# Attention on one core: four heads scored earlier, masks and normalising on GpSimd, half of the key copy by DMA

## The reference

```python
proj = h @ w_in
oa = _dilated_attention(...)            # heads 0-7: softmax of q k^T / 8 - slope * distance + log(count)
# heads 8-15, in blocks of 128 queries
sc = jnp.einsum("bhqe,bhke->bhqk", q_i, k) * (dh ** -0.5)
sc = sc + c_i[..., None] - c[:, :, None, :]
sc = jnp.where(kpos[None, :] <= qpos[:, None], sc, -jnp.inf)
p = jax.nn.softmax(sc, axis=-1)
o = jnp.einsum("bhqk,bhke->bhqe", p, vf)
return jnp.concatenate([oa, ob], axis=-1) @ w_out
```

## Time and profile before

| | us |
|---|---|
| median of 3 runs | 1294.28 (1294.25 to 1295.91) |
| the profiled execution | 1295.59 |
| its span in the trace | 1293.8 |
| TensorE busy | 1254.6 (97%) |
| VectorE busy | 936.4 (72%) |
| ScalarE busy | 769.2 (59%) |
| GpSimd busy | 294.9 (23%) |
| mean granted clock of TensorE | 0.989 |

### The profile page before, as it was taken

The page is one execution under the profiler, slowest core; times in us unless marked ns, Lnnn a source line. Parts: engine busy times, 40 slices in busy tenths (PEclk is TensorE's granted clock), DMA queues, the critical chain, the costliest instruction groups (busy, mean ns, idle before and its releaser), DMA issues.

```text
span 1293.8 us, 19412 instructions
## 1 busy us (share of the span) xinstructions
PE 1254.6 (97%) x7446; PEld 1101.4 (85%) x7446; DVE 936.4 (72%) x1223; ACT 769.2 (59%) x1064; POOL 294.9 (23%) x303
## 2 busy tenths in 40 slices
PE   9988986899999999999999999999999999999997
PEld 6766775689899898998989889898889899898996
DVE  6366447569967859588866697657799876959678
ACT  6666465347757456576546564646668746557564
POOL 2554341011122111220222121142212221111220
PEclk9999998999999999999999999999999999999999
DMA  7355446577899898996586867968598999898983
GB/s 249 83 115 122 122 106 138 136 207 198 193 218 222 216 233 202 219 202 207 112 206 148 227 140 209 210 136 191 154 239 182 215 230 232 214 231 183 218 220 102
DMA packets 148492, 238.96 MB, mean 185 GB/s; under 512 B 51616, under 2 KB 73384, under 8 KB 148400
## 3 DMA queue, kind: packets, MB, share of 16 engines
q0 software_dynamic: 32352, 102.79, 42.2%
q1 hardware_dynamic: 115744, 134.60, 33.2%
q10 hardware_dynamic: 304, 0.33, 0.1%
HBM read 127.57 MB, written 2.11 MB: 100 GB/s over the span
## 4 chain that ended last, share of the span: by engine, by line
PE 87%; DVE 6%; ACT 2%; issue 2%; DMA 1%; POOL 1%; SPq 0%; DVEq 0%; ACTq 0%; POOLq 0%
PE bank L899 21%; PE bank L931 18%; PE bank L1306 11%; PE bank L1374 6%; PE pv L931 5%; PE bank L1256 5%; PE pv L899 4%; PE bank L1097 4%; PE bank L1037 3%; PE bank L1198 2%; PE bank L1064 2%; DVE arena L2250 1%; PE bank L1270 1%; PE bank L1320 1%; PE pv L1320 1%
## 5 line engine op out<-in xcount | busy, mean ns | idle before, releaser
L2167 DVE TENSOR_TENSOR w<-raw_tiles,w 128x1024 fp32r<-128x1024 f32 x312 | 371.5, 1222 | 90.9 <-ACT w L1516 90.8
L1516 ACT ACTIVATE w<-raw_tiles 128x1024 fp32r<-128x1024 f32 x312 | 315.2, 1051 | 123.8 <-PE bank L931 59.9
L3080 POOL DMA_DIRECT2D raw_tiles<-raw_tiles x176 | 152.2, 907 | 629.3 <-DVE w L2167 376.3
L899 PE MATMUL bank<-h_ops,w 128*128 128x256 f32 x2304 | 281.4, 283 | 0.0
L899 PEld LDWEIGHTS bank<-h_ops,w 128*128 128x128 f32 x2304 | 278.9, 192 | 0.7
L931 PE MATMUL bank<-w,arena_q 128*128 128x512 f32 x1044 | 241.5, 390 | 0.0
L931 PEld LDWEIGHTS bank<-w,arena_q 128*128 128x128 f32 x1044 | 195.2, 188 | 40.5 <-DVE x L2469 0.3
L1306 PE MATMUL bank<-w,h_ops 128*128 128x512 f32 x624 | 144.0, 390 | 0.0
L1306 PEld LDWEIGHTS bank<-w,h_ops 128*128 128x128 f32 x624 | 116.6, 188 | 24.0
L1097 PE MATMUL bank<-hT_hi,w 128*128 128x512 f32 x224 | 78.5, 401 | 0.1
L1735 ACT ACTIVATE arena<-arena,negmax 128x512 f32<-128x512 f32 (+1 forms) x64 | 35.9, 561 | 58.4 <-DVE negmax L2250 58.0
(11 more groups left out here) (252 smaller groups left out, 1836.4 us busy)
## 6 DMA issues: line engine op xcount, KB each, us to landing
raw_tiles<-raw_tiles POOLq DMA_DIRECT2D x176, 512.0 KB, 5.5
raw_tiles<-in_ffn_w_in SPq DMA_DIRECT2D x64, 512.0 KB, 5.6
raw_tiles<-in_ffn_w_out SPq DMA_DIRECT2D x64, 512.0 KB, 6.4
raw_tiles<-in_odd_w_in SPq DMA_DIRECT2D x32, 512.0 KB, 5.4
raw_tiles<-in_even_w_in SPq DMA_DIRECT2D x48, 256.0 KB, 3.3
raw_tiles<-in_odd_w_in SPq DMA_DIRECT2D x32, 256.0 KB, 5.4
raw_tiles<-in_odd_w_out SPq DMA_DIRECT2D x16, 512.0 KB, 6.0
raw_tiles<-raw_tiles POOLq DMA_DIRECT2D x20, 256.0 KB, 4.4
```

What stands on the lines that cost most here:

```text
L899: mm = pe.matmul(bank[first + b][:, 256 * m:256 * m + 256], w_slots[use_slot(use)][:, p, k, c:c + P], h_ops[:, H_BLOCK[op], q, k, :], star ...
L1516: nc.scalar.activation(w_flat(use_slot(use), 0, half), raws[tile][:, 1024 * half:1024 * half + 1024], ACT.Copy).then_inc(m_hi, 1)
L2167: nc.vector.tensor_tensor(w_flat(use_slot(use), 1, half), raws[use_tile(key)][:, 1024 * half:1024 * half + 1024], w_flat(use_slot(use), 0, ...
L3080: pool.dma_start(raws[dst][:, part], raws[src][:, part], accum_op=ALU.add).then_inc(t_made[value][half], 16)
```

## The change

- **Steps.** Heads 8 to 11 are scored beside jobs 16 to 19, head 12 right behind its key job 22, so two heads instead of three are left to the tail.
- **Buffers.** Two of `rden` and of the output `o_sb`; heads 13 and 15 have part and turned buffers of their own (`OWN`); `v_rest` has a place for each group; the mask of the first block goes to `first_block`.
- **Masks and normalising** move from VectorE to GpSimd, but for the last pair. The factor 1/P_SCALE moves to the output's high and low part.
- **Key copy.** For pairs 0 to 5 ScalarE writes each head's own half, and two DMAs on SP's queue write the other half. The first score unit of a head waits for them (`key_copied`).
- **Order in a step.** VectorE makes the first logits before the parts and the output's low part last. TensorE turns the output at piece 5 instead of 0.
- **`early_split`** would put a weight split between the exponentials; it returns False for every job.

```diff
-         15: [(None, 7, 6, 2)],
-         16: [(None, None, 7, None)],
-         17: [(None, None, None, 3)],
-         18: [(8, None, None, None)],
-         19: [(9, 8, None, None)],
-         21: [(10, 9, 8, None)],
-         22: [(11, 10, 9, None)],
-         23: [(12, 11, 10, 4)],
-         24: [(13, 12, 11, None), (14, 13, 12, 5), (15, 14, 13, None)]}
+         15: [(8, 7, 6, 2)],
+         16: [(9, 8, 7, None)],
+         17: [(10, 9, None, 3)],
+         18: [(11, 10, None, None)],
+         21: [(None, None, 8, None)],
+         22: [(12, 11, 9, None)],
+         23: [(13, 12, 10, 4)],
+         24: [(14, 13, 11, None), (15, 14, 12, 5)]}
-TAIL = [(None, 15, 14, 6), (None, None, 15, None), (None, None, None, 7)]
+TAIL = [(None, 15, 13, None), (None, None, 14, 6), (None, None, 15, None), (None, None, None, 7)]
+OWN = (13, 15)
+COPIED_PAIRS = 6
+def early_split(j):
+    return False
...
             def step(h, g, v, pair):                       # VectorE
-                if g is not None:
-                    parts_lo(g, 0)
                 if h is not None:
                     logits(h, 0)
                 if g is not None:
-                    parts_lo(g, 1)
-                    parts_lo(g, 2)
-                if h is not None:
-                    logits(h, 1)
...
-                if pair is not None:
-                    output_lo(pair)
+                    for u in range(3):
+                        parts_lo(g, u)
                 if v is not None:
                     value_sum(v)
                 if h is not None:
+                    logits(h, 1)
                     logits(h, 2)
-                if v is not None and v % 2 == 1:
-                    normalise(v // 2)
+                if pair is not None:
+                    output_lo(pair)
...
+            def copy_keys(pair):                           # SP
+                sp.wait_ge(aev, e_aev(e_job_of(pair, 1)))
+                for head, own in enumerate(ROWS):
+                    sp.dma_start(k_stack[ROWS[1 - head], pair % 2, head, :].bitcast(F32),
+                                 k_stack[own, pair % 2, head, :].bitcast(F32)).then_inc(key_copied, 16)
...
                     quarter(n + 2, q, e_panel(n + 2)[2 * q:2 * q + 2])
+                    if E_PANELS[n][0] == "qk" and q % 2 and 2 * E_PANELS[n][1] + q // 2 < COPIED_PAIRS:
+                        copy_keys(2 * E_PANELS[n][1] + q // 2)
...
                 if u == 0:                                 # TensorE, scores_unit
-                    pe.wait_ge(lev, e_lev(e_job_of(h // 2, 1)))
+                    pe.wait_ge(lev, e_lev(e_job_of(h // 2, 1)) + (h == NHEAD - 1))
+                    if h // 2 < COPIED_PAIRS:
+                        pe.wait_ge(key_copied, 32 * (h // 2 + 1))
...
-                if n == 0 and pair is not None:            # TensorE, attention
-                    turn_output(pair)
+                if n == (0 if h == 14 else 1) and v is not None:
+                    gather_values(v)
                 if n in (0, 3, 6) and h is not None:
                     scores_unit(h, n // 3)
-                if n == 1 and v is not None:
-                    gather_values(v)
+                if n == 5 and pair is not None:
+                    turn_output(pair)
...
+            def first_masks(h):                            # GpSimd
+                pool.wait_ge(bias_landed[h % 2], 16 * ((h - 8) // 2 + 1))
+                mask(h, TT - 1)
+                pool.wait_ge(logit_ready, 4 * h)
+                mask(h, 0, first_block[:, :])
+            def later_masks(h):
+                pool.wait_ge(logit_ready, 4 * h + 1)
+                mask(h, 2)
+                pool.wait_ge(logit_ready, 4 * h + 2)
+                mask(h, 1)
+            def normalise(pair):
+                pool.wait_ge(rden_ready, pair + 1)
+                pool.wait_ge(o_summed, 2 * (pair + 1))
+                heads = o_sb[pair % 2].rearrange("p (k n) -> p k n", k=8)
+                nc.gpsimd.tensor_tensor(heads, heads, rden[:, pair % 2, :]...to_broadcast([P, 8, HD]),
+                                        ALU.mult).then_inc(o_norm, 1)
```

More of the change, by code:

```diff
@@ L334, with same_parts_before, landed_count @@
 POOL_PANELS = range(2, 7)
+def same_parts_before(h):
+    if h == 0 or h == 8 or h in OWN:
+        return None
+    return h - 1 if h < 8 else h - 2
+def early_split(j):
+    return False
+def landed_count(h):
+    return OWN.index(h) + 1 if h in OWN else h + 1 - sum(own < h for own in OWN)
 def value_count(j):
@@ L603, in trunk @@
         p_landed = [sem(f"p_landed{u}") for u in range(3)]
+        p_own = [sem(f"p_own{u}") for u in range(3)]
+        key_copied = sem("key_copied")
         value_rest = sem("value_rest")
@@ L1796, in _ @@
                             else:
-                                for rows in ROWS:
+                                for rows in ROWS if pair >= COPIED_PAIRS else (own,):
                                     last = nc.scalar.activation(k_stack[rows, st, head, :], src[own, :], ACT.Copy)
@@ L1804, in _ @@
                     for st in STEPS.get(j, []):
-                        step(*st)
+                        step(*st, j + 1 if early_split(j + 1) else None)
                 if n == 0:
@@ L2254, in logits @@
                     col += n
-                    if h >= 8 and tb:
-                        mask(h, tb - 1)
             def parts_lo(g, u):
@@ L2336, in _ @@
                         key_lo(j, 0)
-                        first, *others = STEPS[j]
-                        step(*first)
-                        for st in others:
+                        dve.wait_ge(aev, e_aev(j))
+                        key_lo(j, 1)
+                        for st in STEPS[j]:
                             step(*st)
@@ L3031, in split_lo, with mask @@
                                         panel_quarter((n + 1) % 2, 0, c).bitcast(F32), ALU.subtract).then_inc(lo_split, 1)
+            def mask(h, tb, dst=None):
+                own = table[:, h % 2, P * tb:P * tb + P]
+                nc.gpsimd.tensor_tensor(own if dst is None else dst, own, causal[:, :], ALU.add).then_inc(mask_made, 1)
+            def first_masks(h):
[11 more added lines that the diff above has]
+                pool.wait_ge(o_summed, 2 * (pair + 1))
+                heads = o_sb[pair % 2].rearrange("p (k n) -> p k n", k=8)
+                nc.gpsimd.tensor_tensor(heads, heads, rden[:, pair % 2, :].rearrange("p (k o) -> p k o", o=1).to_broadcast([P, 8, HD]),
+                                        ALU.mult).then_inc(o_norm, 1)
             for c in range(4):
```

218 lines of the change are left out of this document (130 added, 88 removed).

## The result

The changed kernel took 1298.86 us (median of 19 runs, 1296.31 to 1301.76) against 1295.36 us before (19 runs): ratio 1.0029, 95% interval 1.0022 to 1.0037, that is 3.5 us more by the medians, 3.8 by the ratio. The forecast was 1292.4, from a median of 1294.28 before. The profiled execution of after has a span of 1296.1 us at a mean clock of 0.99, against 1293.8.

A forecast was written before the change was run, and what follows sets the result against it. It took a ring through ScalarE and VectorE, not TensorE, to set the pace in the steps of heads 1 to 7; 7.0 - 4.0 + 4.9 - 9.7 = -1.8 from the median 1294.28 gave 1292.4 us, range 1283 to 1300.

The forecast's parts named there:

- Part 1: First head: TensorE waits 5.9 us for pair 0's DMA key copies, plus half clock 1.3; +7.0 us, ends 5.2 and 7.9.
- The bounds for the landing: Pair 0's key copies land between 61.0 (2.0 us after the second issue) and 62.3 (3.3 after); 61.6 taken.
- hidden: Steady steps after pair 0: the DMA key copies cost nothing, since the copied keys are wanted a whole job later.
- Part 2: Steps of heads 1 to 7: shorter key copies and new order shorten five turns by 0.8 us; -4.0, ends -1 and -8.
- the case that I had priced at 0.2 a turn: Heads 1 to 7: GpSimd's tensor operation gets between VectorE's three parts; last logits end at 8.2 instead of 8.4.
- The collision that I had named: GpSimd's tensor operations and VectorE's two-operand parts keep each other out; two parts took 1.95 us instead of 1.36.
- Part 3: Heads 8 to 11, steps 15 to 18, to job 24's end: masks behind GpSimd's split; +4.9 us, ends 0 and +9.
- The wait of 3.2 for the transposes in step 17: Step 17: TensorE waits 3.2 us for the transposes of pair 3.
- Part 4: Tail: one head less scored, 34.8 us against 44.5, with waits of 6.5; -9.7 us, ends -6 and -13.
- Rival (b): GpSimd's queue becomes the bound from step 11, masks and normalising behind the split; +4.5 us, 1298.8, chance 0.24.
- the signs listed: First-head wait 5 to 6.5 us, logits of heads 8 to 11 awaiting masks, head 12 wait about 3, tail 33 to 36.
- the ring: Steps of heads 1 to 7: a loop through ScalarE and VectorE, not TensorE, sets the pace, 10.1 to 10.4 us a turn.

The follow-up runs named there:

- e5: Changed kernel with pair 0's keys written by ScalarE alone, pairs 1 to 5 still by DMA behind the weight loads; 1288.15 us, ratio 0.9945.
- e2: Changed kernel with the two key copies issued on SP ahead of the same quarter's weight loads; 1289.24 us, ratio 0.9952.
- e1: Changed kernel with all key copies written by ScalarE again, no DMA copy; 1294.39 us, ratio 0.9995.
- e7: Changed kernel with key copies ahead of the weight loads, GpSimd's log-count table addition left out for heads 0 to 7; 1285.1 us, ratio 0.9917.
- e6: Changed kernel with key copies ahead of the weight loads, and early_split true for jobs 8 to 19; 1269.78 us, ratio 0.9803.
- e3: Changed kernel with masks and normalising back on VectorE, DMA copies kept; 1301.03 us, ratio 1.0042.
- e12: Changed kernel with copies ahead of loads, early split, GpSimd's last weight split late, and masks and normalising back on VectorE; 1281.11 us, ratio 0.9897.

## Why the prediction was wrong

By its terms, against the table of cuts:

- **Part 1, +7.0 for the key copy.** This is the step that failed. It had the right cause, pair 0's copies on SP behind the loads, and sized both of its terms too low. Measured by after against e5: 6.6 us to head 0 and 3.4 more from there to head 7, +10.0, outside the ends of 5.2 and 7.9. (The bounds for the landing, 61.0 and 62.3, would give 6.4 and 7.7 by the same working.) The wait was 7.14 where the working gave 5.9. I had bounded issue to landing by 2.0 and 3.3 us, which fits the copy by itself (median 2.3 in e2), and left out the two loads of 256 KB issued just ahead of it: behind them it took 4.1. The half clock was put at 1.3; work ran at 0.50 from 63.28 to about 68.6, which loses 2.7. For the later pairs "hidden" was right for the time only: four waits of 9.1 us do stand in the trace, and e5 shows that they cost nothing.
- **Part 2, -4.0 for the turn.** With the first head out of the way (e5) heads 0 to 7 take 66.3 against 70.4: -4.1. Right in size, and partly by luck. By e1 the new order on VectorE, with the normalising on GpSimd, gives nothing without the shorter copy (71.5), so all of it is ScalarE's. In the turns of heads 1, 2, 3 and 5 GpSimd did get between the parts (2.72 us instead of 1.62), the case that I had priced at 0.2 a turn; and 2.4 of the 4.1 us lie ahead of head 3. The collision that I had named costs 4.5 us in all (e7).
- **Part 3, +4.9 to the end of job 24.** Measured from head 7's first logits: 88.1 or 88.2 against 82.9, +5.3. Right in the sum. The waits at head 12 (3.33 us, forecast 3.15) and at the last scores of step 18 (2.46, forecast 2.9) were there. The wait of 3.2 for the transposes in step 17 was not; in its stretch stand two waits on the copies, at heads 8 and 10 (2.79 and 2.60), which I had counted as hidden.
- **Part 4, -9.7 for the tail.** Between the cuts it is -7.6 (36.3 against 43.8), but the two tails do not hold the same work. Before its last transposes the old one makes 45 + 18 = 63 output products, the new one 48 + 24 = 72 (groups by shape in each tail: busy us, mean ns, idle before):

```profile
L1037 PE MATMUL bank<-w,arena_r 128*128 128x512 f32 x45 | 13.9, 439 | 0.0
...
L1037 PE MATMUL bank<-w_raw,arena_r 128*128 128x512 f32 x18 | 5.6, 434 | 0.0
```
```profile
L1092 PE MATMUL bank<-w,arena_r 128*128 128x512 f32 x48 | 13.8, 413 | 0.0
L1092 PE MATMUL bank<-w_raw,arena_r 128*128 128x512 f32 x24 | 7.1, 409 | 0.0
```

  Nine products are about 2.1 us (an estimate from nine of them in 2.3), work that is then missing behind the transposes: from their start to the end of the span it is 1037.4 us after and 1038.8 before. At equal work the tail gave 9.0 to 9.7, so this price was right. Its terms: waits 6.0 against 6.5, and after the wait of 3.93 us the clock was down for 3.3 us of work (235.9 to 239.1), which loses 1.6 where 0.8 was allowed.
- **early_split, nothing.** True as a statement on the edit. It hid the largest term in this code: 19 us (e6).

The measured parts give +10.0 - 4.1 + 5.3 - 7.6 = +3.6 up to the last transposes; behind them 1.4 come back, which leaves the 2.3 by which the spans differ. Against the -1.8 of the forecast the traces are off by 4.1, of which Part 1 has 3.0 and Part 3 0.4; up to 0.7 lie in the tail and behind it. The other 1.2 us, up to the +3.5 of the runs, are the distance of the profiled runs from their medians. With 10.0 in the place of 7.0 the forecast's own sum is +1.2, and its sign turns. The rest of it held: without Part 1 it comes to -8.8, and e5, the change without pair 0's DMA, measured -7.1 by its ratio.

Rival (b) gave 1298.8, the measured time, and that was luck: it had GpSimd's masks cost 2 us more in Part 3 and 3 in Part 2, and neither was seen, while e3 shows that taking them off GpSimd gains nothing. Of the signs listed, the waits at the first head and at head 12 were there, the first of them 7.1 and not 5 to 6.5. VectorE's first logits waited for GpSimd's mask at heads 8 and 9 (1.41 and 0.56 us), not at 10 and 11. The tail (36.3, or 36.9 to the transposes' end) is past the upper end of 33 to 36, by the nine products.

Open: how the collisions share out in the steps of heads 8 to 11, and what of e12's 16 us is masks and what normalising. Neither was run by itself. Nor was the early split without its effect on the collision, so the 19 us are not shared out between the two.

## What to carry to other kernels

Before moving work to a DMA, ask where in its queue the issue stands at its first use: here five steady uses cost nothing and the first cost 10 us, since TensorE had nothing else to do, the copy landed later behind fresh loads, and the work after it ran at half clock. A wait that is named in a list is not yet a cost: 9 us of them vanished with no gain that the runs can see, because the ring behind them set the pace. And before a stretch is compared between two versions, count the work in it: here nine products had moved across the cut. When a ring of two engines sets the pace, look for the piece of it that could stand in one of the engines' holes; moving 1 us there gave 19, and the traces show that it also drew two colliding engines apart.

## What the runs showed of the hardware

A copy of 128 KB within SBUF took 4.1 us from issue to landing when it was issued behind two loads of 256 KB, and 2.3 when issued ahead of them (e2, medians of 12). In after that is longer than a load of 256 KB from memory takes. The DMA issues of after (count, KB each, median us to landing):

```profile
raw_tiles<-in_even_w_in SPq DMA_DIRECT2D x48, 256.0 KB, 3.5
...
arena_q<-arena_q SPq DMA_DIRECT2D x12, 128.0 KB, 4.1
```

TensorE's clock stayed at the lower level for more than 5 us of steady work after a wait of 7.14 us. And a TENSOR_TENSOR on GpSimd of 1024 columns made an operation of 0.69 us on VectorE last 2.31 (e12); one of 512 columns added 1.1 us to three parts (2.72 for 1.62 to 1.63).
